# Leaving 25 full-width TensorE products whose sums nobody reads out of each layer's mixing stage

## The reference, cut to what matters

```python
def step(S, inp):                       # RWKV-7, per token, forward and backward
    r_t, w_t, k_t, v_t, kk_t, a_t = inp
    sa = jnp.einsum('bhij,bhj->bhi', S, -kk_t)
    S = (S * w_t[:, :, None, :] + sa[..., None] * (kk_t * a_t)[:, :, None, :]
         + v_t[..., None] * k_t[:, :, None, :])
    return S, jnp.einsum('bhij,bhj->bhi', S, r_t)
...
def one_block(qi):                      # differential attention, 128 queries
    s = jnp.einsum('bhqcd,bhkcd->bhcqk', qi, k).astype(jnp.float32) * scale
    p = jax.nn.softmax(s, axis=-1)
    p = p[:, :, 0] - lam * p[:, :, 1]
    return jnp.einsum('bhqk,bhkd->bhqd', p.astype(v.dtype), v)
```

## Time and profile before

| | |
|---|---|
| median of 3 runs | 4365.92 us (4365.31 to 4370.72) |
| the profiled execution | 4365.16 us, span of the core 4363.4 us |
| mean granted TensorE clock over the span | 0.958 of 2.4 GHz |
| PE matmul busy | 4046.7 us, 93% of the span |
| DVE / ACT / POOL busy | 3395.8 / 1586.1 / 1398.7 us |
| mixing stage, first layer (about 338 to 632 us) | PE busy 46 to 47 of each 50 us between 395 and 545 us |

### The profile page before, as it was taken

One profiled execution on the slowest core, in us unless ns is written; L12 is line 12 of the kernel. 1 busy time (PEld: TensorE's weight loads), 2 busy tenths in 40 slices (PEclk: granted clock), 3 DMA queues, 4 the chain that ended last, 5 costly groups with the idle time before them and its releaser, 6 DMA issues. The chain is left out here.

```text
span 4363.4 us, 71520 instructions
## 1 busy us (share of the span) xinstructions
PE 4046.7 (93%) x26630; PEld 3240.7 (74%) x26630; DVE 3395.8 (78%) x6371; ACT 1586.1 (36%) x2620; POOL 1398.7 (32%) x1046
## 2 busy tenths in 40 slices
PE   7999988999998999999979899799999899999996
PEld 5977767765577888888879677586656688888885
DVE  2556753689898999999855576448898899999996
ACT  4425543211284333333353355321114633333333
POOL 0010000154305666666400000004441166566661
PEclk8988998999999999999989799899999999999998
DMA  6220012599889999999721300237997999999994
GB/s 243 73 112 19 2 46 102 162 350 337 292 255 365 409 409 404 405 405 404 308 88 54 125 2 2 93 107 265 308 353 254 276 408 409 409 405 403 405 407 176
DMA packets 412900, 1096.19 MB, mean 251 GB/s; under 512 B 38240, under 2 KB 183904, under 8 KB 405984
## 3 DMA queue, kind: packets, MB, share of 16 engines
q1 hardware_dynamic: 265184, 555.88, 35.6%
q0 software_dynamic: 147456, 536.94, 31.7%
HBM read 1013.25 MB, written 79.43 MB: 250 GB/s over the span
## 5 line engine op out<-in xcount | busy, mean ns | idle before, releaser
L1747 POOL DMA_INDIRECT ring<-peer_u_rows,rows x512 | 662.9, 1295 | 1985.1 <-DVEq L2098 1180.1
L1747 POOL DMA_INDIRECT ring<-peer_v,rows x512 | 711.2, 1389 | 411.7 <-DVE acc L2558 338.1
L1704 PE MATMUL ps<-h,u 128*128 128x384 f32 x2048 | 677.2, 487 | 2.5 <-PEq L1819 2.5
L204 PE MATMUL ps<-vhi,wlo 128*128 128x512 f32 x1536 | 609.7, 397 | 70.4 <-DVE wlo L2537 67.9
L2558 DVE SCALAR_TENSOR_TENSOR acc<-ring,act,acc 128x1024 f32<-128x1024 f32 x508 | 644.4, 1278 | 24.2 <-DMA ring<-peer_v,rows 20.3
L1751 DVE SCALAR_TENSOR_TENSOR ring<-ring,acc 128x1024 f32<-128x1024 f32 x512 | 619.0, 1222 | 25.2 <-DMA ring<-peer_u_rows,rows 16.8
L205 PE MATMUL ps<-vlo,whi 128*128 128x512 f32 x1536 | 605.2, 394 | 0.0
L206 PE MATMUL ps<-vhi,whi 128*128 128x512 f32 x1536 | 605.0, 394 | 0.0
L1704 PEld LDWEIGHTS ps<-h,u 128*128 128x128 f32 x2048 | 383.0, 190 | 252.0 <-issue 3.1
L204 PEld LDWEIGHTS ps<-vhi,wlo 128*128 128x128 f32 x1536 | 292.9, 191 | 145.1 <-issue 85.2
L204 PE MATMUL ps<-xhi,ulo 128*128 128x384 f32 x1024 | 344.9, 337 | 23.2 <-DVE xlo L2515 23.2
(11 more groups left out here) (358 smaller groups left out, 7383.4 us busy)
## 6 DMA issues: line engine op xcount, KB each, us to landing
u<-peer_u SPq DMA_DIRECT2D x256, 512.0 KB
v<-peer_v SPq DMA_DIRECT2D x256, 512.0 KB
gates<-stage SPq DMA_DIRECT2D x24, 2048.0 KB, 9.6
sel<-gates SPq DMA_DIRECT2D x64, 768.0 KB
mod_ring<-mod_late SPq DMA_DIRECT2D x32, 1024.0 KB, 7.8
query_raw<-peer_wq SPq DMA_DIRECT2D x64, 512.0 KB
hidden<-hh SPq DMA_DIRECT2D x128, 192.0 KB
u<-hidden SPq DMA_DIRECT2D x128, 192.0 KB
```

What stands on the lines that cost most here:

```text
L204: pe.matmul(out, lhs[1], rhs[0], start=start, stop=False)
L1704: mm = pe.matmul(self.g.ps[:, bank, 0:ND], self.u[:, slot, kc, :], self.x[:, kc, 0:ND], start=(kc == 0), stop=(kc == KC - 1))
L1747: return pool.indirect_dma_start(to, None, table, rows)
```

## The change

The function `fill` and its calls are taken out. Nothing else moves: no wait, no buffer, and no instruction of another engine changes. PE's list is 25 products shorter in the body of the layer loop.

```diff
@@ -1202,10 +1202,6 @@
             units = [(dr, c, h, slice(h * HD, (h + 1) * HD)) for dr in range(2) for c in range(CA) for h in range(2)]
-
-            def fill(bank):
-
-                pe.matmul(g.ps[:, bank, 0:CA * P], g.ident, g.proj[:, Q0, 0:CA * P], start=True, stop=True)
 
             def hop(name, step, added):
@@ -1370,10 +1366,6 @@
                     pe.wait_ge(state_in, 32)
                 hop(name, step, nx)
-                if name in ("rhs0", "rhs1", "sa0", "sa1"):
-                    fill(C)
-                elif name == "state0":
-                    fill(A)
                 nx += name in XSUMS
```

## The result

The changed kernel takes 4394.26 us (median of 4 runs, 4391.4 to 4397.19); the kernel before, beside it, 4366.98 us (median of 4). The ratio is 1.0061, 95% interval 1.0044 to 1.0079: 27 us slower, where the forecast was 4367 us and the range ended at 4386 us. The profiled execution has a span of 4389.6 us, 26.2 us more than before.

The account below looks back on a forecast made before the run. PE was taken as the bound, 93% busy, with the clock at risk. Per layer, 4.2 us saved against clock losses of 3.0 and 2.1 gave +0.9, +1.8 in all: 4367 us, range 4354 to 4386.

Parts of the forecast that it names:

- What the missing products give back: Steps 0 to 4: PE time saved of 0, 0.1, 1.8, 2.0 and 0.4 us, taken as 4.2 us a layer.
- No gap follows: Step 3: attention units are short, so four removed products save about 0.5 us each; 2.0 us in all.
- The gaps grow and the waits stay: Idle gaps widen to about 1.45 us (step 0), 2.1 (step 1), 2.0 (before rhs1, step 4); DVE and ACT start no earlier.
- In steps 0 and 2 the gaps grow to 1.5 us, 2.5 of 4 us busy: like the row that held: Steps 0 and 2: clock stays up, as at 360 to 364 us, where PE was busy 2.48 of 4 us.
- The price of a fall: Time lost when the clock drops to 1.2 GHz: bounds 0 and 3.5 us, 3.0 us taken in step 1.
- At the end of step 4: Clock drop likely around rhs1 and sa1, slowing state1 by 2.1 us a layer.
- The fall before step 4: Existing clock drop behind 588 us, left unchanged in the forecast; avoiding it would save another 3.5 us a layer.
- One of the two stretches of step 1 falling, because a slower PE fills the second: Step 1, behind sa0 or around sa1: one clock drop a layer, costing 3.0 us.
- The sum: Per layer -4.2 + 3.0 + 2.1 = +0.9 us, over two layers +1.8 us.
- the slower rival: Gaps in steps 0 and 2 also lose the clock; six places a layer, 15.9 us a layer, 4397.0 us; chance 0.27.
- it decides from the third fall a layer: Three clock drops in steps 0 to 2 give 6.9 us a layer, 4379.0 us; two stay within 0.2%.
- the one row I preferred: Stretch 360 to 364 us, PE busy 2.48 of 4 us without losing the clock; taken as evidence for steps 0 and 2.

Follow-up runs that it names:

- the run without the 8 products: Against the kernel before, products removed only behind sa0, state0, sa1 of step 2, rhs0, sa0, rhs1, sa1 of step 3, rhs0 of step 4; 4364.4 us.
- with eight products: Against the kernel before, only 8 of 25 products a layer stay: behind sa0 and sa1 of steps 0 to 2, rhs0 and rhs1 of step 1; 4379.7 us.
- the quarter product: Against the kernel before, each product uses 64 rows and 64 columns of the array, with the same 256 columns of data; 4382.3 us.

## Why the prediction was wrong, point by point

- **What the missing products give back: right in kind, sized too high.** Forecast 4.2 us a layer, measured 3.07: step 2 gave 0.59 + 0.48 + 0.59 = 1.66 (forecast 1.8; the last of the three is read in the run without the 8 products, since in the changed kernel the clock fell there), step 4 0.40 (0.4), step 1 0.11 (0.1; with eight products, 2.62 us in place of 2.73), but step 3 only 0.20 + 0.43 + 0.22 + 0.05 = 0.90 in place of 2.0. "No gap follows" did not hold there: with the products gone PE ran into waits for DVE and for ACT's exponentials, gaps of 0.2 to 0.5 us that the products had covered.
- **The gaps grow and the waits stay: right.** 1.34 us for 1.45, 2.11 for 2.1 in step 1, 1.97 for 2.0 before `rhs1` of step 4, each with the releaser of before.
- **"In steps 0 and 2 the gaps grow to 1.5 us, 2.5 of 4 us busy: like the row that held": this step failed.** The clock fell in both steps, behind stretches of 2.6 of 4 us busy. I compared by idle time alone, with one row. These are the gap in that row and a longer one, both in the kernel before:

```profile
363.26 1.15 PE L1240 MATMUL ps<-pwt,px 64*64 64x64 f32 x32 [1.52 <-ACT pwt L1424]
...
472.24 0.69 PE L1227 MATMUL ps<-proj,ar 64*64 64x64 f32 x32 [1.61 <-DVE mk L1453]
```

  The first, between rows of small products, did not lose the clock in any of the 26 passes profiled here, and the second in none of the 24 in which it stood at full clock, while gaps of 0.9 to 1.34 us at rhs and sa did. What PE did around the gap matters as well, and the quarter product shows one part of it; a rule that sorts the gaps was not found.
- **The price of a fall, 3.0 us and at most 3.5: too low.** Where scores, turns and the whole of `state` follow, a hop of 6.13 us takes 10.0 to 10.6 us and one of 5.63 us takes 7.9 to 9.9; the fall behind `sa0` of step 1 cost 4.5 us in the first layer and 5.5 us in the second over the hops that it reached. In step 2 it is 0.3 to 1.8 us a hop in the two profiles of the changed kernel. The forecast took its bound from a stretch of 10 us at the low clock, and in step 1 the stretches were longer:

```profile
450.50:464.10 13.60, 13.60 (x105) 10.34 (x103) 7.12 (x13) 5.03 (x11) 0.00 (x0) 0.50 0.00 0
2600.90:2618.00 17.10, 17.10 (x126) 12.91 (x127) 7.69 (x16) 6.48 (x14) 0.00 (x0) 0.50 0.01 2
```

  At the end of step 4 it was 2.0 to 2.3 us for a forecast 2.1, in every pass without products.
- **A term that the sum lacks.** The fall before step 4 was taken as unchanged. It begins earlier and lasts 13.6 us in place of 10.2, and the way from `state1` of step 3 to the take of `rhs0` of step 4 is 1.4 us longer in both layers.
- **"One of the two stretches of step 1 falling, because a slower PE fills the second": right in the first profile** (sa0 in both layers, sa1 undisturbed), wrong in the first layer of the second (both, 4.2 us each). The reason given fits the six passes of kernels without products in step 1: in three the low clock lasted into rhs1 (13.6 and 17.1 us) and the second stretch held; in two it ended after 10.2 us, in one `sa0` had not fallen at all, and in these three the second fell.
- **The sum.** In the first profile the hops of the first layer give 12.1 us and those of the second 14.7 us, less 1.1 us that step 0 is shorter between its first take and rhs0: 25.7 of the 26.2 us. By the forecast they were 0.9 us each. The falls of steps 0 to 2 account for most of the difference: with what the missing products give back there, these steps are 9.7 and 12.3 us longer (the early fall of step 3 is in the second number) where +1.1 was forecast. This is the slower rival, "it decides from the third fall a layer", to which I gave 0.27. Its 4397.0 us for six falls at 3.0 us is near the 4394 by two errors against each other: there were three to four falls, and they cost more each. The rule of the Trainium skill, Perfetto Trace Analysis, section Matmul Optimizations, that matmuls should run back to back, was the better guide in steps 0 to 2 than the one row I preferred.

## What to carry to other kernels

Work without a reader can still pay: before a product that "nobody reads" is removed, look at the granted clock around it and at which wait stands behind it, for in a wait it costs nothing, and at the low clock the PE work that follows takes 1.7 times as long (4.39 us for 2.60). A row in which the clock held is evidence for its own mix of instructions, not for another with the same idle time. And the same reading finds gains: fill the gap before the stretch that runs at half clock (here 2.7 us a layer), and remove the fillers that no wait hides (1.3 us a layer).

## What the runs showed of the hardware that I had not expected

With TensorE busy for 2.61 and 2.66 of 4 us, the first with products on 64x64 of the array, the second on all of it, the clock went to 1.2 GHz in the first case and stayed at 2.4 GHz in the second. Two gaps of 0.51 and 0.89 us close together were enough to lose it, and in one profile single gaps of 0.92 us with PE busy 3.08 of 4 us, while single gaps of 1.52 and 1.61 us among the preparing hops never were. Why these hold it is open; widening them was not tried. And one kernel's falls move between executions: the hop from sa1 to state1 of step 0 took 6.13 us in one profile of the changed kernel and 10.13 us in the other.
